# Stick-breaking attention with two copies of its split weights and another order of the steps on three engines

## The reference

```python
z = jnp.einsum('bhqd,bhkd->bhqk', qb, kb).astype(jnp.float32) * scale
mask = s[None, :] < t[:, None]
log_1m = jnp.where(mask, jax.nn.log_sigmoid(-z), 0.0)
between = lax.cumsum(log_1m, axis=3, reverse=True) - log_1m
w = jnp.where(mask, jnp.exp(jax.nn.log_sigmoid(z) + between), 0.0)
outs.append(jnp.einsum('bhqk,bhkd->bhqd', w.astype(vb.dtype), vb))
```

## Time and profile before

| | us |
|---|---|
| median of three timed executions | 3160.93 (3158.85 to 3162.08) |
| the profiled execution | 3153.38 |
| its span | 3151.7 |
| TensorE busy with matmuls | 2991.8 (95%) |
| VectorE busy | 1692.1 (54%) |
| ScalarE busy | 1167.2 (37%) |
| GpSimd busy | 620.9 (20%) |
| mean granted TensorE clock | 0.987 |

### The profile page before, as it was taken

The page is one execution under the profiler, slowest core; times in us unless marked ns, Lnnn a source line. Parts: engine busy times, 40 slices in busy tenths (PEclk is TensorE's granted clock), DMA queues, the critical chain, the costliest instruction groups (busy, mean ns, idle before and its releaser), DMA issues.

```text
span 3151.7 us, 40804 instructions
## 1 busy us (share of the span) xinstructions
PE 2991.8 (95%) x14682; PEld 2475.8 (79%) x14682; DVE 1692.1 (54%) x2737; ACT 1167.2 (37%) x2047; POOL 620.9 (20%) x365
## 2 busy tenths in 40 slices
PE   5999989999999999878899999989999999899999
PEld 5888878888888888667788888777788877777887
DVE  5555567554565334788541113367476633865763
ACT  2222223222232222466432222363544434545442
POOL 0000002010000000100334443302422233052223
PEclk9999999999999999999999999999999999999999
DMA  5555531555535233200222232302211232032113
GB/s 203 179 177 178 173 119 53 188 185 169 173 115 172 97 103 100 75 16 12 67 81 93 94 106 93 114 27 67 95 47 54 87 106 83 14 104 65 53 47 108
DMA packets 88603, 322.51 MB, mean 102 GB/s; under 512 B 10256, under 2 KB 11024, under 8 KB 87824
## 3 DMA queue, kind: packets, MB, share of 16 engines
q1 hardware_dynamic: 64992, 233.65, 22.8%
q0 software_dynamic: 19488, 71.31, 6.6%
q10 hardware_dynamic: 3984, 15.64, 1.4%
HBM read 312.18 MB, written 6.29 MB: 101 GB/s over the span
## 4 chain that ended last, share of the span: by engine, by line
PE 59%; issue 23%; DVE 8%; POOL 6%; DMA 2%; ACT 1%; ACTq 0%; POOLq 0%; SPq 0%; DVEq 0%
PE psum L376 49%; POOL w_lo L357 6%; PE psum L2114 3%; PE psum L1042 2%; PE psum L695 1%; PE psum L1012 1%; PE psum L444 1%; PE psum L433 1%; DVE small L1088 1%; DVE ada_acc L681 1%; DVE pt_lo L1107 1%; DVE tb L495 1%; DMA ada_first<-ada_in 1%; DVE h_lo L504 1%; DMA ada_raw<-ada_in 1%
## 5 line engine op out<-in xcount | busy, mean ns | idle before, releaser
L357 POOL TENSOR_TENSOR w_lo<-raw,w_hi 128x1024 fp32r<-128x1024 f32 x219 | 533.6, 2444 | 1597.1 <-ACT w_hi L331 1415.0
L376 PE MATMUL psum<-h_hi,w_hi 128*128 128x512 f32 x1824 | 500.1, 401 | 28.0 <-DVE h_lo L504 11.6
L376 PE MATMUL psum<-h_hi,w_lo 128*128 128x512 f32 x1824 | 486.6, 393 | 0.0
L376 PE MATMUL psum<-h_lo,w_hi 128*128 128x512 f32 x1824 | 486.5, 393 | 0.0
L376 PEld LDWEIGHTS psum<-h_hi,w_hi 128*128 128x128 f32 x1824 | 346.1, 191 | 116.9 <-DVE h_lo L504 17.8
L376 PEld LDWEIGHTS psum<-h_lo,w_hi 128*128 128x128 f32 x1824 | 343.7, 188 | 75.6
L376 PEld LDWEIGHTS psum<-h_hi,w_lo 128*128 128x128 f32 x1824 | 344.2, 189 | 74.5
L345 ACT ACTIVATE w_hi<-raw 128x1024 fp32r<-128x1024 f32 x256 | 257.9, 1048 | 161.1 <-DMA raw<-stream_in 161.1
L351 DVE TENSOR_TENSOR w_lo<-raw,w_hi 128x1024 fp32r<-128x1024 f32 x192 | 227.8, 1222 | 111.2 <-ACT w_hi L345 104.8
L331 ACT ACTIVATE w_hi<-raw 128x1024 fp32r<-128x1024 f32 x177 | 185.6, 1053 | 207.2 <-PE psum L376 110.7
L821 ACT ACTIVATE a_hi<-tb 128x512 f32 (+1 forms) x88 | 55.6, 632 | 546.3 <-DVE tb L866 546.3
(11 more groups left out here) (453 smaller groups left out, 4788.6 us busy)
## 6 DMA issues: line engine op xcount, KB each, us to landing
raw<-stream_in SPq DMA_DIRECT2D x433, 512.0 KB, 3.7
ada_raw<-ada_in POOLq DMA_DIRECT2D x128, 512.0 KB, 4.7
ada_first<-ada_in POOLq DMA_DIRECT2D x2, 2048.0 KB, 20.8
ada_first<-ada_in SPq DMA_DIRECT2D x2, 2048.0 KB, 26.1
x_held<-X ACTq DMA_DIRECT2D x2, 2048.0 KB, 6.8
X<-x_held ACTq DMA_DIRECT2D x2, 2048.0 KB, 7.8
X<-xT_in ACTq DMA_DIRECT2D x1, 2048.0 KB, 9.7
out_x<-X SPq DMA_DIRECT2D x8, 256.0 KB, 2.9
```

Of the source, the lines that this page charges most:

```text
L357: pool.tensor_tensor(w_lo[:, u % RING], raw[:, u % RAW], w_hi[:, u % RING].bitcast(F32), ALU.subtract).then_inc(lo_ready, 1)
L376: mm = pe.matmul(dst, w[wi], m[mi], start=(first and n == 0), stop=(last and n == total - 1), skip_group_check=skip)
```

## The change

The keys of pairs 0 and 1 become one tensor `ka` in which a pair's high and low parts lie together: the first 2048 columns are all that pair 0 has. When heads 0 and 1 have their scores, that place is free, and the second copy of the split weights goes there: `wt_hi1` with 1280 columns and `wt_lo1` with 768. The remaining 512 low columns, `wt_lo1_last`, lie in the temporary area behind `sb_t`. Even heads use copy 0, odd heads copy 1. `split_weights` of a head waits for the values of two heads before, and makes the low part of an odd step of an odd head in two instructions, as its place is in two parts.

The order changes on all three engines. TensorE: `accumulate(m)` now precedes `values`. ScalarE: `logarithms(m + 1)` precedes `weigh(m - 1)`. VectorE: `softpluses(m)` is followed by `split_weights(m - 2)`, with the last two at the end. `out` and `sb_out_act` come two steps later, so that those of pairs 2 and 3 both stand after the loop. Ahead of the stage, the four zeroings of `ka` cover low parts first and high parts then, and in layer 0 the third waits for the copy of `crr`.

```diff
--- before.py
+++ after.py
@@ -1563,8 +1563,8 @@
         crr = at("crr", [P, NCONSTR, P], F32R)
         crf = at("crf", [P, 2, P])
         hybrid = top[0]
-        ka_hi = at("ka_hi", [P, 2, 2, S], F32R)
-        ka_lo = at("ka_lo", [P, 2, 2, S], F32R)
+        ka_base = top[0]
+        ka = at("ka", [P, 2, 2, 2, S], F32R)
         va_hi = at("va_hi", [P, 4, 4, 3, 64], F32R)
         va_lo = at("va_lo", [P, 4, 4, 3, 64], F32R)
         za = at("za", [P, 4, S])
@@ -1572,8 +1572,20 @@
         SB_AT, SB_ALL = {3: 0, 2: P, 1: 3 * P, 0: 6 * P}, 10 * P
         sp_hi = at("sp_hi", [P, 2, SB_ALL], F32R)
         sp_lo = at("sp_lo", [P, 2, SB_ALL], F32R)
-        wt_hi = at("wt_hi", [P, SB_ALL], F32R)
-        wt_lo = at("wt_lo", [P, SB_ALL], F32R)
+        WT_LAST = SB_AT[0]
+        wt_hi = [at("wt_hi0", [P, SB_ALL], F32R),
+                 nc.alloc_sbuf_tensor_at("wt_hi1", [P, SB_ALL], F32R, offset=ka_base)]
+        wt_lo0 = at("wt_lo0", [P, SB_ALL], F32R)
+        wt_lo1 = nc.alloc_sbuf_tensor_at("wt_lo1", [P, WT_LAST], F32R, offset=ka_base + 4 * SB_ALL)
+        wt_lo1_last = nc.alloc_sbuf_tensor_at("wt_lo1_last", [P, S], F32R, offset=ta_base + 4 * SB_ALL)
+
+        def weights_low(h, span):
+
+            if h % 2 == 0:
+                return wt_lo0[:, span]
+            if span.start >= WT_LAST:
+                return wt_lo1_last[:, span.start - WT_LAST:span.stop - WT_LAST]
+            return wt_lo1[:, span]
         sb_t = nc.alloc_sbuf_tensor_at("sb_t", [P, SB_ALL], F32, offset=ta_base)
         sb_w = nc.alloc_sbuf_tensor_at("sb_w", [P, SB_ALL], F32, offset=sq_base)
         assert top[0] <= nc.sbuf_usable_end, (top[0], nc.sbuf_usable_end)
@@ -1888,8 +1900,9 @@
 
         def sb_keys(pair):
 
-            hi, lo = (ka_hi, ka_lo) if pair < 2 else (keys_hi, keys_lo)
-            return hi[:, :, pair % 2], lo[:, :, pair % 2]
+            if pair < 2:
+                return ka[:, pair, 0], ka[:, pair, 1]
+            return keys_hi[:, :, pair % 2], keys_lo[:, :, pair % 2]
 
         def sb_pe(pe, L):
             def z(m):
@@ -1933,7 +1946,8 @@
                 for wi, mi in ((0, 0), (1, 0), (0, 1)):
                     for j in range(4):
                         v = (va_hi, va_lo)[wi][:, j, h // 2, h % 2:h % 2 + 2, :].rearrange("p a n -> p (a n)")
-                        mm = pe.matmul(bank(g)[:, j * P:S], v, (wt_hi, wt_lo)[mi][:, SB_AT[j]:SB_AT[j] + S - j * P],
+                        span = slice(SB_AT[j], SB_AT[j] + S - j * P)
+                        mm = pe.matmul(bank(g)[:, j * P:S], v, weights_low(h, span) if mi else wt_hi[h % 2][:, span],
                                        start=(n == 0 and h % 2 == 0), stop=(n == 11 and h % 2 == 1),
                                        skip_group_check=True)
                         n += 1
@@ -1942,9 +1956,9 @@
             z(1)
             for m in range(16):
                 z(m + 2)
+                accumulate(m)
                 if m % 2 == 1 and m >= 3:
                     values((m - 3) // 2)
-                accumulate(m)
             values(7)
 
         def sb_act(act, order, L):
@@ -1980,12 +1994,13 @@
             logarithms(0)
             for m in range(16):
                 exps(m + 1)
+                logarithms(m + 1)
                 if m:
                     weigh(m - 1)
-                logarithms(m + 1)
-                if m % 4 == 2 and m >= 6:
-                    sb_out_act(act, L, (m - 6) // 4)
+                if m % 4 == 0 and m >= 8:
+                    sb_out_act(act, L, (m - 8) // 4)
             weigh(15)
+            sb_out_act(act, L, 2)
             sb_out_act(act, L, 3)
 
         def sb_out_act(act, L, p):
@@ -2007,12 +2022,20 @@
                 softplus.give(dve.tensor_tensor(lo, t, hi.bitcast(F32), ALU.subtract), (L, m))
 
             def split_weights(m):
-                if m % 2 == 0 and m:
-                    dve.wait_ge(prod.sem, prod.at(("sb", L, m // 2 - 1)))
+                h = m // 2
+                if m % 2 == 0 and h >= 2:
+                    dve.wait_ge(prod.sem, prod.at(("sb", L, h - 2)))
                 dve.wait_ge(weights.sem, weights.at((L, m)))
-                w, hi, lo = sb_w[:, sb_all(m)], wt_hi[:, sb_all(m)], wt_lo[:, sb_all(m)]
-                order.step(dve.tensor_copy(hi, w))
-                weights_lo.give(dve.tensor_tensor(lo, w, hi.bitcast(F32), ALU.subtract), (L, m))
+                order.step(dve.tensor_copy(wt_hi[h % 2][:, sb_all(m)], sb_w[:, sb_all(m)]))
+                spans = [sb_all(m)]
+                if m % 4 == 3:
+                    spans = [slice(spans[0].start, WT_LAST), slice(WT_LAST, SB_ALL)]
+                for n, span in enumerate(spans):
+                    op = dve.tensor_tensor(weights_low(h, span), sb_w[:, span], wt_hi[h % 2][:, span].bitcast(F32),
+                                           ALU.subtract)
+                    if n + 1 < len(spans):
+                        order.link(op)
+                weights_lo.give(op, (L, m))
 
             def out(p, phase):
                 g = own[L, "sbg", p]
@@ -2028,13 +2051,15 @@
                                                    ALU.subtract), (L, "ya", p))
             for m in range(16):
                 softpluses(m)
-                if m:
-                    split_weights(m - 1)
-                if m % 4 in (2, 3) and m >= 6:
-                    out((m - 6) // 4, m % 4 - 2)
+                if m >= 2:
+                    split_weights(m - 2)
+                if m % 4 < 2 and m >= 8:
+                    out((m - 8) // 4, m % 4)
+            split_weights(14)
             split_weights(15)
-            out(3, 0)
-            out(3, 1)
+            for p in (2, 3):
+                out(p, 0)
+                out(p, 1)
 
 
         def nsa_attention(l):
@@ -2649,7 +2674,9 @@
                 split_lo(dve, u + c + LEAD)
                 if c < 4:
                     rows, side = SIDES[c % 2]
-                    order.link(dve.memset((ka_hi, ka_lo)[c // 2][rows, 1 - side].bitcast(F32), 0.0))
+                    if l == 0 and c == 2:
+                        dve.wait_ge(part_hi.sem, part_hi.at("crr"))
+                    order.link(dve.memset(ka[rows, :, 1 - c // 2, 1 - side].bitcast(F32), 0.0))
                     evac_split_dve(dve, g + c, ya_hi[:, c], ya_lo[:, c], 0.125)
                     continue
                 if c == 6:
```

## The result

The changed kernel takes 3144.2 us (median of five, 3135.9 to 3146.5) against 3159.6 us (3155.8 to 3162.1) of the kernel before: ratio 0.9946, 95% interval 0.9935 to 0.9957, so 17.1 us faster (13.6 to 20.5); the two medians alone differ by 15.4. The forecast was 3143.3 us, from a gain of 17.6.

What follows compares the result with a forecast made beforehand. A ring of waits between VectorE, TensorE and ScalarE, none full, bounds the stage in both hybrid layers; cutting it saves 8.1 us in layer 0 and 9.5 in layer 1, so 3160.93 - 17.6 = 3143.3 us, range 3134 to 3153.

Steps and rivals of the forecast that it cites:

- The ring: Odd accumulate, ScalarE's exponentials, VectorE's split queued ahead of the next softplus, that softplus: waits closing at 8.0 us a head.
- The lanes: Each engine's own timeline through the stage, laid out in the new order; layer 0 reaches the dense matmuls 8.1 us sooner.
- TensorE's 7.13 a head: TensorE's gapless work per head in the stage, against 8.00 us from one odd accumulate to the next before.
- VectorE's 6.85: VectorE's work per head in us, softpluses and weight splits, once its 1.07 us idle ahead of the odd split goes.
- 7.45 with gating: VectorE's us per head once the gating of finished pairs adds one instruction of 0.60 to a head.
- The two-part split: Low weights of odd steps of odd heads in two VectorE instructions: 0.07 us dearer each, 8 times, 0.6 in all.
- The clock, the term that was off: Low TensorE clock at the stage's end, charged at 1.66 us in the new tail as in the old.
- The tail from the last softplus to the dense matmuls: End of the stage, softplus(15) to the first dense matmul: forecast at about 7.2 us.
- Gating, two steps later: Two pairs left for the stage's end instead of one, beside values(7): costs nothing, up to 1.0 us if not.
- A: Rival: ring cut but engines don't pack, 0.5 us a head lost in 14 heads; gain 10.6, 3150 us; chance 0.16.
- C: Rival: clock stays low in the stage's steady part, 7.1 us more per such head; 3172 at four heads; chance 0.05.
- D: Rival: no effect, another wait closes the ring at 8 us; 3158 to 3162 us; chance 0.08.

Runs made afterwards that it cites:

- the second profile: The changed kernel, unaltered, profiled and timed once more: ratio 0.9945 to the kernel before, stages 67.3 and 67.3 us.
- the fillers: Changed kernel plus 20 throw-away matmuls on TensorE in the idle stretch ahead of accumulate 15: ratio 0.9933 to the kernel before, stages 66.7 and 66.7 us.

## Why the prediction was right

*The ring.* Read from three timelines of one head, it gave the wait to cut and its length. The run with the split one step behind shows it.

*The lanes.* In layer 0 the forecast put accumulate 3 at 15.6 us after the start, accumulate 13 at 51.7, accumulate 15 at 59.3 (its times less 2061.76). Measured 15.6, 51.7 and 59.2; in the second profile accumulate 3 was at 16.4 and accumulate 15 at 59.5. TensorE's 7.13 a head was 7.02 to 7.08, VectorE's 6.85 was 6.90 with the two-part split in it, 7.45 with gating was 7.43 to 7.51. The handing over from TensorE's lane to VectorE's came where it was forecast.

*The two-part split.* 1.08 us (2088.50 to 2089.58) against 1.01 for one instruction: 0.07, as taken. (The Trainium skill, VectorE: DVE Perf Modes, section on the TRN2 errata, would give 0.16 as an estimate; by its fit a 512-column instruction lasts 0.69, and the trace has 0.68, so the length agrees. The price is less, as the second starts 0.08 us before the first has ended, 2088.98 against 2088.50 + 0.56.)

*The clock, the term that was off.* I charged the new end 1.66 us a layer for the low clock, as much as the old one paid. It fell low again after a like idle, on the accumulate and the values behind it, but most of that lay beside VectorE's split: the fillers show 0.5 and 0.7 us. The old 1.66 had 1.39 of it in the dense matmuls, and of that 0.1 is left (2.07 us for the first eight instead of 3.39). The tail from the last softplus to the dense matmuls, forecast at 7.2, was 8.1 and 7.8, and 7.3 with fillers. That so little was paid is in part luck: where the clock fell sooner behind such an idle (the runs with ScalarE's order or the gating as before), the stage paid 1.0 us more, which would have brought the charge close to the forecast's. Without a clock charge the sum for the new layer 0 was 66.5, and with fillers it is 66.7. The forecast was therefore 1 us a layer too small in the stages, 19.5 in place of 17.6, counting the dense matmuls behind them. The total of 17.1 can't tell these apart, so that it met the forecast within 1 us is luck as well: the profiled execution, forecast at 3135.8, took 3143.1.

*Gating, two steps later.* "Nothing" was right as to the end: it lies beside the last values. What I did not see is that the old place would have cost 2.1 to 2.6 us with the other orders changed. The sum was right because the lanes were laid out with the new places.

*The rivals.* A, half the gain, didn't come: behind the start the logarithm made VectorE wait once, 0.17 us in layer 1 ahead of softplus 5, and not at step 9, where the forecast had its thinnest margin. C didn't come, with the clock at 1.00 through the middle. (The short idles in which the Trainium skill, TensorE: Matmul & The Clock Gate, section on psum-queue depth-cycling, sees the clock swing are not there any more, and where they were, in the earlier trace rows, the clock was 1.00 too.) D didn't come either: no head took longer than 7.51 us.

*Left open.* The parts outside the stages scatter by up to 10 us from one profiled execution to the next. Where in them was not followed up. Totals of the variants with one copy and with TensorE's old order are 4 to 7 us better than their stages; for the latter the low clock in layer 1's one profile (3.95 us) may be part of it. So I trust the stages for a ranking and the totals for the main result only.

## What to carry to other kernels

When three engines are each busy 60 to 85% and none is full, write one period of each as a list of steps with start to start times and follow who waits for whom around the ring: the step to move is the one that is queued ahead of work that doesn't need it. Such a move takes a buffer and an order together, and the experiment that takes either away gives nothing. Then lay the new lanes out from the start to the last step, as the end (here 8 of 67 us) follows other rules than the middle.

## What the runs showed of the hardware

The throw-away matmuls of 128 columns with one and the same weights ran 0.11 us apart (36 in 4.18 us) at a granted clock of 1.00. The trace has a weight load for each of them (36), so the same weights were loaded again each time.

The low clock behind an idle stretch need not be paid for: in the changed kernel it slowed accumulate 15 and the values of head 6, and keeping it away gained 0.5 and 0.7 us. What counts is whether TensorE is what is late just then, and where the fall lands: behind idles of 2.6 to 2.95 us accumulate 15 took from 2.5 to 3.9 us (the changed kernel twice, ScalarE's order and the gating as before), where 2.1 is the full clock's. Behind 1.16 and 1.40 us, with the last softplus sooner, the granted clock stayed at 1.00.
